# Memory attention in rounded products, with its value products one slot later: a one-core encoder kernel on Trainium2

## What is computed

```python
def _memory_branch(q_raw, mem, w_kv):
    B, S, _ = q_raw.shape
    M = mem.shape[1]
    q = q_raw.reshape(B, S, MEM_HEADS, MEM_HD)          # 256 x 4 x 256
    kv = (mem @ w_kv).reshape(B, M, 2, MEM_HEADS, MEM_HD)
    k, v = kv[:, :, 0], kv[:, :, 1]
    s = jnp.einsum('bqhd,bmhd->bhqm', q, k).astype(jnp.float32) * (MEM_HD ** -0.5)
    p = jax.nn.softmax(s, axis=-1).astype(v.dtype)
    return jnp.einsum('bhqm,bmhd->bqhd', p, v).reshape(B, S, MEM_WIDTH)
```

## Time and profile before

| | |
|---|---|
| time, median of 3 runs | 1706.89 us (1706.84 to 1707.12) |
| the profiled execution: time, span from first to last instruction | 1706.24 us, 1704.5 us |
| TensorE busy | 1699.0 us |
| VectorE busy | 1168.3 us |
| ScalarE busy | 815.7 us |
| DMA, mean over the span | 233 GB/s |
| granted TensorE clock | 1.000 |

### The profile page before, as it was taken

One profiled execution on the slowest core, in us unless ns is written; L12 is line 12 of the kernel. 1 busy time (PEld: TensorE's weight loads), 2 busy tenths in 40 slices (PEclk: granted clock), 3 DMA queues, 4 the chain that ended last, 5 costly groups with the idle time before them and its releaser, 6 DMA issues.

```text
span 1704.5 us, 20450 instructions
## 1 busy us (share of the span) xinstructions
PE 1699.0 (100%) x8694; PEld 1411.7 (83%) x8694; DVE 1168.3 (69%) x1024; ACT 815.7 (48%) x674; POOL 94.1 (6%) x87
## 2 busy tenths in 40 slices
PE   9999999999999999999999999999999999999999
PEld 8888888898888888888888888888888888888886
DVE  4854566678877655545666679888989798655445
ACT  4454445454545445444444526554554555443332
POOL 0000002222222100000000000000000000000000
PEclk9999999999999999999999999999999999999999
DMA  9676776455665687667888958778787876878553
GB/s 363 240 251 209 253 242 210 174 172 184 184 208 197 198 248 270 214 213 252 256 269 278 360 198 255 242 230 260 237 243 252 240 236 180 261 239 306 198 197 124
DMA packets 137370, 397.98 MB, mean 233 GB/s; under 512 B 22336, under 2 KB 51392, under 8 KB 122816
## 3 DMA queue, kind: packets, MB, share of 16 engines
q1 hardware_dynamic: 129568, 377.15, 66.0%
q0 software_dynamic: 2720, 10.49, 3.3%
q10 hardware_dynamic: 4992, 9.05, 1.4%
HBM read 365.06 MB, written 30.93 MB: 232 GB/s over the span
## 4 chain that ended last, share of the span: by engine, by line
PE 99%; DVE 0%; ACT 0%; issue 0%; POOL 0%; DVEq 0%; POOLq 0%
PE pair L2145 21%; PE pair L2146 21%; PE pair L2147 21%; PE pair L2417 4%; PE pair L2415 4%; PE pair L2416 4%; PE pair L2119 3%; PE side L2397 3%; PE side L2395 3%; PE side L2396 3%; PE pair L2117 1%; PE pair L2397 1%; PE pair L2396 1%; PE pair L2395 1%; PE side L2227 1%; PE pair L2129 1%
## 5 line engine op out<-in xcount | busy, mean ns | idle before, releaser
L1396 DVE TENSOR_TENSOR weight_lo<-raw,weight_hi 128x2048 fp32r<-128x2048 f32 x210 | 481.0, 2292 | 396.2 <-ACT weight_hi L974 393.6
L974 ACT ACTIVATE weight_hi<-raw 128x2048 fp32r<-128x2048 f32 x210 | 402.3, 1916 | 520.1 <-DMA raw<-in_stream 519.9
L2145 PE MATMUL pair<-weight_hi,act_both 128*128 128x512 f32 x928 | 368.5, 397 | 0.6 <-DVE weight_lo L1396 0.6
L2147 PE MATMUL pair<-weight_hi,act_both 128*128 128x512 f32 x928 | 361.6, 390 | 0.0
L2146 PE MATMUL pair<-weight_lo,act_both 128*128 128x512 f32 x928 | 361.4, 389 | 0.0
L2145 PEld LDWEIGHTS pair<-weight_hi,act_both 128*128 128x128 f32 x928 | 174.3, 188 | 37.0 <-issue 1.0
L2147 PEld LDWEIGHTS pair<-weight_hi,act_both 128*128 128x128 f32 x928 | 174.2, 188 | 36.7
L2146 PEld LDWEIGHTS pair<-weight_lo,act_both 128*128 128x128 f32 x928 | 174.3, 188 | 35.3
L1295 ACT ACTIVATE part_hi<-part_raw 128x2048 fp32r<-128x2048 f32 x60 | 113.7, 1912 | 123.6 <-DVE part_raw L1887 49.8
L1867 DVE TENSOR_TENSOR part_lo<-part_raw,part_hi 128x2048 fp32r<-128x2048 f32 x60 | 136.4, 2281 | 42.7 <-ACT part_hi L1295 42.6
L2145 PE MATMUL pair<-weight_hi,ff_both 128*128 128x512 f32 x352 | 136.9, 389 | 0.0
(11 more groups left out here) (320 smaller groups left out, 2546.4 us busy)
## 6 DMA issues: line engine op xcount, KB each, us to landing
raw<-in_stream SPq DMA_DIRECT2D x256, 1024.0 KB, 5.5
part_raw<-in_stream SPq DMA_DIRECT2D x30, 1024.0 KB, 6.9
part_raw<-in_stream POOLq DMA_DIRECT2D x10, 1024.0 KB, 10.7
scratch<-spill ACTq DMA_DIRECT2D x32, 256.0 KB, 5.1
ln_rows<-in_ln_rows SPq DMA_DIRECT2D x6, 1024.0 KB, 8.3
gate<-scratch SPq DMA_DIRECT2D x12, 512.0 KB, 6.9
ff_scratch<-ff_blocks SPq DMA_DIRECT2D x11, 512.0 KB, 6.6
ff_land<-ff_scratch SPq DMA_DIRECT2D x44, 128.0 KB, 5.5
```

Source lines behind the costliest of these rows:

```text
L974: act.activation(hi_of(n), raw_of(n), ACT.Copy).then_inc(extra_h if extra(n) else h_ready, 1)
L1396: dve.tensor_tensor(lo_of(n), raw_of(n), hi_of(n).bitcast(F32), ALU.subtract)\
L2145: pe.matmul(out, hi[:, k0 + k, tok], w_hi[:, k, :], start=first and k == 0, stop=False)
L2147: mm = pe.matmul(out, lo[:, k0 + k, tok], w_hi[:, k, :], start=False, stop=last and k == 3)
```

## The change

The memory attention's scores and value products, each made so far of full float32 matmuls, are made of three rounded matmuls each. For that ACT copies `qm_land`, `k_mem` and `v_mem` to `qm_hi`, `km_hi` and `vm_hi` in slots 108, 109 and 110, and DVE makes `qm_lo`, `km_lo` and `vm_lo` in the same slots; `vm_hi` lies where `qm_land` lay and so waits for `qm_lo`. The scores of unit 8 wait for `km_lo`. The probabilities of units 8 to 11 get a `p_hi` (the ACT copy that was `prob_t`) and a `p_lo`, which DVE makes in slot s+7, and their value products stand behind piece s+7 instead of s+6, the taking of the result in slot s+8 (`valued_at`). The read of the next unit's blocks waits for `p_lo`. The reads of `k_mem` and `v_mem` move up by one load each. The first branch piece waits for `yh_l` alone, the second group of pieces for the latent attention's units, the third for all 12. The semaphores `q_rotated`, `k_rotated` and `kz_done` become steps of one, `rotated`.

```diff
+    qm_hi = at("qm_hi", 120, [NB, T], F32R)
+    qm_lo = at("qm_lo", 144, [NB, T], F32R)
+    km_lo = at("km_lo", 128, [NB, T], F32R)
+    vm_lo = at("vm_lo", 136, [2, TT, 512], F32R)
+    vm_hi = at("vm_hi", 152, [2, TT, 512], F32R)
+    km_hi = at("km_hi", 188, [NB, T], F32R)
...
+        def valued_at(n, later):
+
+            u = unit_at(n, later + 6)
+            if u is not None and u < HEADS:
+                return u
+            u = unit_at(n, later + 7)
+            return u if u is not None and u >= HEADS else None
...
                     if u:
                         sp.wait_ge(pt_done, u)
+                    if u > HEADS:
+                        sp.wait_ge(p_lo_done, u - HEADS)
...
-            loads(HG_END + 6, HG_END + 10)
+            loads(HG_END + 6, HG_END + 9)
 
             sp.wait_ge(yh_l, 1)
-            for k, (unit, dst) in enumerate(((U_KM, k_mem[:].rearrange("p (u b) t -> p u (b t)", b=2)),
-                                             (U_VM, v_mem[:].rearrange("p j t c -> p (j t) c")))):
-                sp.dma_start(dst, scratch[unit:unit + 4].rearrange("u p c -> p u c")).then_inc(mem_back, 16)
-                load(Nth(HG_END + 10 + k))
-                carry_prob(HG_END + 10 + k)
-            loads(HG_END + 12, HG_END + 13)
+            for k, (unit, dst, back) in enumerate(((U_KM, k_mem[:].rearrange("p (u b) t -> p u (b t)", b=2), k_back),
+                                                   (U_VM, v_mem[:].rearrange("p j t c -> p (j t) c"), v_back))):
+                sp.dma_start(dst, scratch[unit:unit + 4].rearrange("u p c -> p u c")).then_inc(back, 16)
+                load(Nth(HG_END + 9 + k))
+                carry_prob(HG_END + 9 + k)
+            loads(HG_END + 11, HG_END + 13)
...
                     for c in range(2):
-                        act.activation(squared(q_mem[:, 4 * c:4 * c + 4, :]), slices(qm_land[:, c]), ACT.Copy)\
-                           .then_inc(qm_ready, 1)
+                        act.activation(squared(qm_hi[:, 4 * c:4 * c + 4, :]), slices(qm_land[:, c]), ACT.Copy)\
+                           .then_inc(mem_split_h, 1)
+                if n == HG_END + 9:
+                    act.wait_ge(k_back, 16)
+                    act.activation(km_hi[:], k_mem[:], ACT.Copy).then_inc(mem_split_h, 1)
+                if n == HG_END + 10:
+                    act.wait_ge(v_back, 16)
+                    act.wait_ge(mem_split_l, 2)
+                    act.activation(vm_hi[:], v_mem[:], ACT.Copy).then_inc(mem_split_h, 1)
...
+                if n == HG_END + 8:
+                    for c in range(2):
+                        dve.wait_ge(mem_split_h, c + 1)
+                        part = (slice(None), slice(4 * c, 4 * c + 4))
+                        dve.tensor_tensor(squared(qm_lo[part]), slices(qm_land[:, c]), squared(qm_hi[part].bitcast(F32)),
+                                          ALU.subtract).then_inc(mem_split_l, 1)
+                if n == HG_END + 9:
+                    dve.wait_ge(mem_split_h, 3)
+                    dve.tensor_tensor(km_lo[:], k_mem[:], km_hi[:].bitcast(F32), ALU.subtract).then_inc(mem_split_l, 1)
+                if n == HG_END + 10:
+                    dve.wait_ge(mem_split_h, 4)
+                    dve.tensor_tensor(vm_lo[:], v_mem[:], vm_hi[:].bitcast(F32), ALU.subtract).then_inc(mem_split_l, 1)
+                u = valued_at(n, 0)
+                if u is not None and u >= HEADS:
+                    dve.wait_ge(pt_done, u + 1)
+                    if u > HEADS:
+                        dve.wait_ge(valued, u)
+                    dve.tensor_tensor(squared(p_lo[:]), prob_land[:].rearrange("p (s k j) -> p k s j", k=2, j=SQ),
+                                      squared(p_hi[:].bitcast(F32)), ALU.subtract).then_inc(p_lo_done, 1)
...
-                u = unit_at(n, 6)
+                u = valued_at(n, 0)
                 if u is not None:
-                    pe.wait_ge(pt_done, u + 1)
+                    if u < HEADS:
+                        pe.wait_ge(pt_done, u + 1)
+                    else:
+                        pe.wait_ge(mem_split_l, 4)
+                        pe.wait_ge(p_lo_done, u - HEADS + 1)
...
                     if u == HEADS:
-                        pe.wait_ge(mem_back, 32)
-                        pe.wait_ge(qm_ready, 2)
+                        pe.wait_ge(mem_split_l, 3)
...
-                                mm = pe.matmul(out, q_mem[:, b, tok], k_mem[:, b, :], start=j == 0, stop=j == 1)
+                                for i, (w, a) in enumerate(((qm_hi, km_hi), (qm_hi, km_lo), (qm_lo, km_hi))):
+                                    mm = pe.matmul(out, w[:, b, tok], a[:, b, :], start=j == 0 and i == 0,
+                                                   stop=j == 1 and i == 2)
...
             for k in range(12):
+                if k == 0:
+                    pe.wait_ge(yh_l, 1)
+                if k == 1:
+                    pe.wait_ge(y_l, HEADS)
+                if k == 2:
+                    pe.wait_ge(y_l, UNITS_ATTN)
```

More of the change, by code:

```diff
@@ L135 @@
 ATTN_SLOTS = [FIRST["q_mem"] + 4 + 4 * u for u in range(HEADS)] + [HG_END + 10 + 3 * u for u in range(MEM_HEADS)]
-assert ATTN_SLOTS[-1] + 7 < FIRST["branch"]
+assert ATTN_SLOTS[-1] + 8 < FIRST["branch"]
 UNITS_ATTN = len(ATTN_SLOTS)
@@ L222, in encoder_program @@
     g_land = at("g_land", 128, [2, 4 * T])
-    q_mem = at("q_mem", 120, [NB, T])
+    qm_hi = at("qm_hi", 120, [NB, T], F32R)
+    qm_lo = at("qm_lo", 144, [NB, T], F32R)
     qm_land = at("qm_land", 152, [2, 4 * T])
@@ L253, in encoder_program @@
     prob_land = at("prob_land", 184, [2 * T])
+    p_hi = at("p_hi", 100.5, [2, T], F32R)
+    p_lo = at("p_lo", 186, [2, T], F32R)
     mem_raw = at("mem_raw", 164, [KD, T])
@@ L360, in encoder_program @@
         c_lo_done = sem("c_lo_done")
-        q_rotated = sem("q_rotated")
+        rotated = sem("rotated")
         two_blocks = sem("two_blocks")
@@ L364, in encoder_program @@
         rope_turned = sem("rope_turned")
-        k_rotated = sem("k_rotated")
-        kz_done = sem("kz_done")
         hg_made = sem("hg_made")
@@ L381, in encoder_program @@
         gates_open = sem("gates_open")
-        qm_ready = sem("qm_ready")
-        mem_back = sem("mem_back")
+        mem_split_h = sem("mem_split_h")
+        mem_split_l = sem("mem_split_l")
+        k_back = sem("k_back")
+        v_back = sem("v_back")
+        p_lo_done = sem("p_lo_done")
         scored = sem("scored")
@@ L1102, in slot @@
                     if i == F_ROWS:
-                        act.wait_ge(kz_done, 1)
+                        act.wait_ge(rotated, 3)
                     take(n, GROUP[name] + c, rows[:], ACT.Copy, 512)
@@ L1155, in slot @@
                 if n == FIRST["k_rope"] + 1:
-                    act.wait_ge(q_rotated, 1)
+                    act.wait_ge(rotated, 1)
                     ended(n)
@@ L1222, in probabilities @@
                         act.wait_ge(valued, u)
-                    act.activation(squared(prob_t[:]), prob_land[:].rearrange("p (s k j) -> p k s j", k=2, j=SQ), ACT.Copy)\
+                    to = prob_t if u < HEADS else p_hi
+                    act.activation(squared(to[:]), prob_land[:].rearrange("p (s k j) -> p k s j", k=2, j=SQ), ACT.Copy)\
                        .then_inc(pt_done, 1)
             def normed_values(n):
-                u = unit_at(n, 7)
+                u = valued_at(n, 1)
                 if u is not None:
@@ L1710, in slot @@
                     dve.wait_ge(trig, 2)
-                    rotate(q_rope[:], 4, 0).then_inc(q_rotated, 1)
+                    rotate(q_rope[:], 4, 0).then_inc(rotated, 1)
                 if n == FIRST["k_rope"] + 2:
                     wait_taken(dve, GROUP["k_rope"])
-                    rotate(rope_x[:, 1:2, :], 1, 1).then_inc(k_rotated, 1)
-                    dve.wait_ge(k_rotated, 1)
+                    rotate(rope_x[:, 1:2, :], 1, 1).then_inc(rotated, 1)
+                    dve.wait_ge(rotated, 2)
                     for h in range(2):
                         last = dve.tensor_scalar(k_rope[:, h, :], rope_x[:, 1, :], head_rows[:, h:h + 1], None, ALU.mult)
-                    last.then_inc(kz_done, 1)
+                    last.then_inc(rotated, 1)
                 if n == HG_END + 3:
@@ L2264, in attention @@
                             for k in range(2):
-                                mm = pe.matmul(side[3][:, b * T:(b + 1) * T],
-                                               v_mem[:, f // 512, k, f % 512:f % 512 + P], prob_t[:, k, :],
-                                               start=k == 0, stop=k == 1)
+                                v = (slice(None), f // 512, k, slice(f % 512, f % 512 + P))
+                                for j, (w, a) in enumerate(((vm_hi, p_hi), (vm_hi, p_lo), (vm_lo, p_hi))):
+                                    mm = pe.matmul(side[3][:, b * T:(b + 1) * T], w[v], a[:, k, :],
```

(7 more changed lines are left out.)

## The result

The changed kernel takes 1709.48 us (median of 21 runs, 1705.88 to 1711.88) against 1706.66 of the kernel before (21 runs on the same chips, 1705.79 to 1707.24): a ratio of 1.0015, 95% interval 1.0008 to 1.0021. It is slower by about 0.15%, where 1707.0 against 1706.9 was forecast, in a range from 1704.5 to 1709.4; it comes out at the upper end of that range. The profiled execution, 1711.88 us with a span of 1710.1, happens to be the longest of the 21; it is used here for the places of the waits, and a second profile, taken later and shorter by 1.43 us, for their size ("The changed kernel again"). One execution of the version with new reads and `p_lo` first took 2857.92 us, at a granted clock of 0.556 over its whole length, and isn't counted in that version's figures.

The account below looks back on a forecast made before the run. TensorE's own work was taken as the bound. Span 1704.5 - 2.3 (matmuls) + 2.3 (wait for `km_lo`) + 0.1 (restart) = 1704.6, with runs 2.4 us above the span: 1707.0 us, range 1704.5 to 1709.4.

Parts of the forecast that it names:

- the band from 1708.2 to 1710.3: Whole kernel: outcome with transfers landing 1 to 2 us later still or `p_lo` late; chance 0.15.
- the forecast's own: Whole kernel: a wait of 1.3 to 3.5 us eats the gain, 1706.0 to 1708.2 us; chance 0.57.
- The matmuls: Memory attention's 8 score and value sets: 1.44 us each instead of 1.73, a gain of 2.3 us.
- The even landings: Four 1 MB transfers (`k_mem`, load 109, `v_mem`, load 110) land 2.6 us apart in order of issue, 657.9 to 665.7.
- The rival in which they come later still: Load 110 lands at 669.0 or later, giving 1710.3 us or more; chance 0.06, and 0.15 for 1708.2 to 1710.3.
- extra of 1 to 2 us: Landing of load 110: a further delay from loads meeting spills, making 1708 to 1709 us.
- The wait for `km_lo` of 2.3 us: Scores of unit 8, due at 675.66, wait on TensorE until `km_lo` is done at 678.0.
- But there is no wait yet: Piece 109: `weight_lo` done at 664.7, TensorE due at 664.78; the 7 us of slack gone, no wait.
- a sign of error: Profile check: the step on the wait is wrong if the gap is at piece 109 or 110 instead.
- That leaves 1.3 us, so I cost it at nothing: Unit 11's value products, slot 126: `p_lo` done at 775.5, TensorE through just ahead of 776.79, no wait priced.
- Gaps ahead of the value products: Profile check: such gaps on TensorE would show the step on the wait to be wrong.
- The rival named this price, 1708.5: Value products wait 0.5 to 2 us each for late `p_lo`, besides the `km_lo` wait: about 1708.5; shares the 0.15.

Follow-up runs that it names:

- the version without waits: Changed kernel with the two reads back at their old place and `p_lo` made ahead of `weight_lo` on VectorE: 1704.35 us, ratio 0.9986.
- keys first: Changed kernel with `km_hi` ahead of ScalarE's rounding of piece 111 and `km_lo` ahead of that piece's `weight_lo`: 1706.99 us, ratio 1.0001.

## Why the prediction was right and wrong

The median of 1709.48 us lies at the upper end of the range (1704.5 to 1709.4). It is in the band from 1708.2 to 1710.3, which had a chance of 0.15, and not in the forecast's own from 1706.0 to 1708.2. The main wait was foreseen with its place and its cause. The sum is 2.5 us short, because two other waits were costed at nothing and TensorE's clock wasn't in it. That the range still reaches the result is luck: it was made wide for the landings, not for these terms.

- **The matmuls**: right. A set takes 1.43 to 1.44 us, and the version without waits shows the whole 2.3 us.
- **The even landings**: right, 2.6 us apart. The rival in which they come later still fell as it was reasoned: the steps between them didn't grow. But load 110 did land 1.2 us later than the forecast (2.0 in the second profile), which is the rival's "extra of 1 to 2 us". What was later was the issue.
- **The wait for `km_lo` of 2.3 us**: right in place, chain and nearly in size, 2.73 us in the profile. `km_lo` was 1.4 us later than reckoned (679.43 for 678.0) and TensorE, held up at piece 109, 1.3 later; the rest is 0.15 us from `km_lo` to the first matmul. Old reads or keys first each take this wait away.
- **"But there is no wait yet" (piece 109)**: wrong by 0.4 to 1.2 us in three profiles of kernels with the new reads, none in two others. The chain had 0.1 us of slack, and it hangs on `yh_lo`, whose time I took as a constant. The issue of `k_mem` came at 652.40 before and at 650.98 to 654.09 in the others, of kernels that are the same up to there. I named a wait at 109 as a sign of error but gave it no price; a slack smaller than the scatter of its source should have been costed at half that scatter. Where the scatter comes from is shown below the list.
- **"That leaves 1.3 us, so I cost it at nothing" (`p_lo` of unit 11)**: the term that failed most, 1.5 to 1.6 us. I compared the new `p_lo` with the due time of the trace before, 776.8. But up to there TensorE saves seven sets, 7 x 0.29 = 2.0 us, and unit 11's own set, 1.73 us, now stands behind the piece instead of ahead of it: TensorE comes 3.7 us earlier, at 773.14 in the run with the old reads. The load on which `p_lo` depended through the queue did not come 3.7 us earlier, but let its `weight_lo` start 1.0 us earlier (771.57 for 772.58), so a slack of 1.3 turned into a wait. Gaps ahead of the value products were the prediction's own sign that it would be wrong. The rival named this price, 1708.5, but at a small chance and for another reason.
- **The clock**: not in the sum at all. About 1.5 us in the one profiled execution that shows it. 10 of the 21 had a granted clock below 1.000, and their mean is 1710.53 against 1707.89 of the other eleven (part of the 2.6 us is longer waits). How many of the ten fell behind the wait isn't shown, since a granted clock of 0.999 doesn't say where it was lost (last section).

The profiles show where the scatter of `yh_lo` comes from. In all twelve it starts 9.76 to 9.78 us behind the start of ScalarE's rounding of piece 106, and that starts when the load of piece 106 has landed, 5.6 to 7.9 us after its issue. ScalarE in the kernel before and in the changed kernel:

```profile
640.32 1.92 ACT L974 ACTIVATE weight_hi<-raw 128x2048 fp32r<-128x2048 f32 x1 [4.51 <-DMA raw<-in_stream]
```

```profile
641.47 1.92 ACT L992 ACTIVATE weight_hi<-raw 128x2048 fp32r<-128x2048 f32 x1 [5.79 <-DMA raw<-in_stream]
```

The wait at piece 109 grows with it. The five profiles with the new reads (us):

| version | rounding of piece 106 | issue of `k_mem` | wait at piece 109 |
|---|---|---|---|
| keys first | 640.17 | 652.27 | none |
| kernel before, new reads | 640.20 | 652.28 | none |
| new reads, `p_lo` first | 640.71 | 652.78 | 0.43 |
| changed kernel | 641.47 | 653.54 | 1.07 |
| changed kernel again | 642.01 | 654.09 | 1.21 |

What moves the landing of piece 106 between executions was not tried.

Put together for the second profile, from the profiled execution before: 1706.24 - 2.35 + 1.21 + 2.74 + 1.57 = 1709.4, against 1710.45 for that execution. Of the 1.0 us between them 0.85 was there ahead of these waits: TensorE was due at piece 109 at 665.63 instead of 664.78. About 0.2 us stays open.

The kernel to keep is the one with the reads at their old place and `p_lo` ahead of `weight_lo`, 1704.35 us, with the value products in either slot.

## What to carry to other kernels

Price a moved step against the new clock of its consumer: each column saved, and each block of work moved behind a wait, brings the consumer to that wait earlier, while what lands by DMA stays where it was. In a queue that runs in order, put the small step that the busiest engine needs next ahead of the large one that it needs two pieces later; this was worth more here than a slot more of distance. And a slack of 0.1 us that hangs on something which scatters by 3 us has to be costed as a wait (three of five profiles showed one here).

## What the runs showed of the hardware

The price of a wait on TensorE isn't only its length. In the first profile of the changed kernel, behind 2.66 us of idleness, the matmuls ran on for some 0.4 us at full rate and then at 0.43 us for 512 columns (1.2 GHz) instead of 0.227 (2.4 GHz) until 683.5. Behind 4.74 us, in the version that waits for `vm_lo`, they did the same until 684.2. Behind 5.20 us they were slow from the first matmul, in the one profile there is; the other four executions of that kernel show the same granted clock, 0.998. But behind 2.67 us in another execution of the changed kernel, and behind 2.45 us in the version with new reads and `p_lo` first, they didn't slow at all. Waits of 0.3 to 1.5 us showed no fall behind them in any profile. What decides between the two outcomes behind the same wait stays open.

The Trainium skill ("TensorE: Matmul & The Clock Gate", What's actually happening) tells of these two rates. The trace agrees: 512 columns at 1.2 GHz are 0.427 us, which is the slow step, and at 2.4 GHz 0.213 us, where the fast one is 0.227.

A granted clock of 0.999 for a whole execution isn't by itself the mark of such a fall. The profiled execution of "keys first" has it, with 1705.76 us and a clock of 1.00 in the whole stage; it was lower only at the very end, where TensorE was all but idle:

```profile
1700.00:1704.00 4.00, 0.16 (x1) 0.00 (x0) 0.86 (x2) 0.00 (x0) 0.00 (x0) 0.77 0.70 229
```

Transfers of 1 MB that SP issued within 1 to 2 us landed in the order of issue and 2.5 to 2.8 us apart, in the kernels before and after. The load of piece 110, fourth in this line instead of second, landed 7.9 us behind the first of them instead of 2.6.
